# Reordering the opening and the schedule of a one-core hybrid attention layer: c turned alone, products of ones, and three ada chunks on TensorE

## The chip, the cores and the metric

The kernel runs on one core of one Trainium2 chip. The metric is the device time of one execution in microseconds. The core has five engines with instruction queues of their own: TensorE (PE), VectorE (DVE), ScalarE (ACT), GpSimd (POOL) and SyncE (SP), the last of which issues nearly all DMAs here. They meet at semaphores only.

## The reference

One layer on x (256 tokens by 1024) with a condition vector c. Everything is float32.

```python
mod = silu(c) @ ada_w + ada_b                     # 1024 x 3072
shift, scale, gate = split(mod, 3)
h = rmsnorm(x, pre_norm_w) * (1 + scale) + shift
mq, mk, mv, mg, dq, dk, dv, dz, db, da = split(h @ w_in)
mq, mk = partial_rope(mq), partial_rope(mk)
o_moba = attention(mq, mk, mv) * silu(mg)         # 8 heads of 64, causal
dq, dk, dv = split(silu(short_conv([dq, dk, dv])))
g = -exp(a_log) * softplus(da + dt_bias); beta = sigmoid(db)
o_dn = gated_delta_rule(dq, dk, dv, g, beta)      # 4 heads of 128, chunks of 64
o_dn = rmsnorm(o_dn, dn_norm_w) * silu(dz)
y = [o_moba, o_dn] @ w_out
out = x + gate * rmsnorm(y, post_norm_w)
```

With 256 tokens the block selection of the attention never picks another block, so it is plain causal attention. The delta rule needs, for each chunk of 64 tokens, the inverse of a lower triangular matrix, and then a recurrence over four chunks.

## The kernel before

Each engine's program is written out by hand as a list of calls of small functions (`hi(5)`, `qkv_products(3)`, `conv(2)` and so on); that list is the order of the work, and waits on semaphores stand in the functions. There is no scheduler.

**Products of high and low parts.** Every large product is done as three products of a reduced float32 type (`three`): high by high, high by low and low by high part. ScalarE rounds a unit of weights to its high part (`hi(n)`, into `whi`), POOL or VectorE takes the difference (`lo(n)`, into `wlo`; `DVE_LO` lists the units whose difference is VectorE's), and TensorE multiplies. There are 44 units: 0 to 15 for q, k, v of the delta rule (two for each of the eight 128-row chunks k of w_in, 768 columns), 16 to 35 for ten groups of 256 other columns of w_in (`half(j)`, two units a group, 1024 columns each), 36 to 43 for w_out (`y_products`). `whi` and `wlo` have four slots, `raw` has five; SP waits for the low part of the unit that had the slot before it loads the next.

**h by quarters.** The shift and scale columns of ada_w come in four quarters of 256 + 256 columns, each in eight chunks of 128 rows. VectorE multiplies the chunks by silu(c) and adds them up (`mod_sums(q, k0, k1)`), TensorE sums over the partitions with a column of ones (`mod(q)`), VectorE makes factor and offset (`modulate(q)`), ScalarE applies them to the turned x (`modulated(q)`) and rounds to `hhi`, VectorE makes `hlo` (`h_lo(q)`). The first quarter's chunks 6 and 7 go to TensorE directly, by one-column products (`mod_direct`, `DVE_K[0] = 6`). Then `qkv_products(2k)` and `(2k+1)` use chunk k of h.

**The opening.** SP loads c and four groups of parameter rows into `prow`, then the constants with the identity, then ada's first quarter, then units. TensorE turns all the rows together (L1252), VectorE copies them and makes the silu of c (L821 to L831), and only then starts `mod_sums(0, ...)`. ScalarE takes both squares of x. x is turned by TensorE (`x_turn`) into banks 0 to 3 and copied by ScalarE.

**After qkv.** VectorE runs the short convolution (`conv(m)`, L886), the gates (`gates_in`, `gates_out`), the silu and the ropes; TensorE meanwhile does the `half(j)` groups. The gated group `half(8)` needs bank and gate of an earlier group (`gate_done`). Then come the decay tables (`rows`, `row_sum`), the inverse in six levels (`z_products`, `mask_z`, `x_products`, `merge`, `t_turn`, alternately for token tiles 0 and 1), the attention heads in between, the recurrence (`vnew_products`, `state_products`, `state_update`), and the w_out products.

## Time and profile before

| | |
|---|---|
| three timed runs | 207.78, 210.75, 211.93 us (median 210.75) |
| profiled execution | 208.55 us, of it 206.5 us span |
| granted TensorE clock, mean | 0.994 |
| VectorE, ScalarE, POOL busy | 127.0, 105.9, 96.5 us |
| first weight product starts | 21.02 us |
| last matmul ends | 200.4 us |
| loaded from memory | 37.04 MB |

The page lists, for each group of instructions, the busy time, the mean of one in ns, and the idle time of its engine before it. In a timeline a row is: start in us, length in us, engine, line, operation, tile written <- tiles read, shapes, count, and in brackets the idle time before it with what ended it. Matmuls overlap, so the pace is read from their starts. A float32 matmul that is not of the reduced type stands as two instructions in the profile.

### The profile page before, as it was taken

To read this page: it belongs to the slowest core of one execution; us is meant where nothing else is said; L and a number is where in the kernel's file an instruction comes from. 1 tells how busy PE (TensorE), PEld (TensorE's weight loads), DVE (VectorE), ACT (ScalarE), POOL (GpSimd) and SP (SyncE) were. 2 spreads that over 40 slices of the span, in tenths; PEclk is the share of its full clock that TensorE was granted. 3 is DMA by queue.
4 is the path that set the end of the run, shared out by engine and by line. 5 is a ranking of instruction groups with operands and counts; after the bars stand their busy time and mean duration, and the time that the engine had idled before them with its cause. 6 is when DMAs were issued, how large, how long until landed. Compare 5 with 4: busy or idle time off the path is not lost.

```text
span 206.5 us, 4647 instructions
## 1 busy us (share of the span) xinstructions
PE 186.6 (90%) x1863; PEld 171.6 (83%) x1863; DVE 127.0 (61%) x306; ACT 105.9 (51%) x197; POOL 96.5 (47%) x51
## 2 busy tenths in 40 slices
PE   0079999999999989999999999999999999999980
PEld 0078999999999879999988999898999787788860
DVE  0634977752169988988586852677795135963055
ACT  4735573546476499965650445335251465545230
POOL 2003385687984927978642039701800480045400
PEclk9999999999999999999999999999999999999997
DMA  6999999994760587289247802450890094020022
GB/s 229 347 362 357 386 357 367 369 383 117 253 205 4 159 171 207 76 124 285 62 109 242 299 12 51 159 205 3 301 396 22 16 312 183 18 83 0 3 102 102
DMA packets 27881, 38.39 MB, mean 186 GB/s; under 512 B 2818, under 2 KB 21459, under 8 KB 27860
## 3 DMA queue, kind: packets, MB, share of 16 engines
q1 hardware_dynamic: 27572, 37.05, 55.6%
q10 hardware_dynamic: 288, 1.05, 1.4%
q8 instruction: 15, 0.25, 0.5%
q14 instruction: 6, 0.05, 0.1%
HBM read 37.04 MB, written 1.05 MB: 185 GB/s over the span
## 4 chain that ended last, share of the span: by engine, by line
PE 80%; DVE 10%; DMA 3%; SPq 2%; ACT 1%; issue 1%; POOL 1%; DVEq 0%; POOLq 0%
PE bank L1243 18%; PE bank L1245 16%; PE bank L1244 16%; DVE cv L886 6%; PE bank L1444 3%; DMA ada<-in_ada_w 3%; PE bank L1455 3%; PE bank L1432 2%; PE bank L1273 2%; PE bank L1266 2%; PE bank L1550 2%; PE bank L1526 2%; PE bank L1492 1%; SPq L322 1%; PE bank L1557 1%; PE bank L1503 1%
## 5 line engine op out<-in xcount | busy, mean ns | idle before, releaser
L442 POOL TENSOR_TENSOR wlo<-raw,whi 128x1024 fp32r<-128x1024 f32 (+1 forms) x30 | 69.6, 2338 | 75.7 <-ACT whi L520 75.7
L1243 PE MATMUL bank<-hhi,whi 128*128 128x256 f32 x224 | 66.0, 295 | 0.5 <-DVE hlo L837 0.5
L1244 PE MATMUL bank<-hhi,wlo 128*128 128x256 f32 x224 | 64.5, 288 | 0.0
L1245 PE MATMUL bank<-hlo,whi 128*128 128x256 f32 x224 | 64.5, 288 | 0.0
L1243 PEld LDWEIGHTS bank<-hhi,whi 128*128 128x128 f32 x224 | 44.1, 197 | 1.7 <-DVE hlo L837 0.9
L1244 PEld LDWEIGHTS bank<-hhi,wlo 128*128 128x128 f32 x224 | 44.2, 197 | 0.0
L1245 PEld LDWEIGHTS bank<-hlo,whi 128*128 128x128 f32 x224 | 44.0, 197 | 0.0
L520 ACT ACTIVATE whi<-raw 128x1024 fp32r<-128x1024 f32 (+1 forms) x33 | 32.8, 1026 | 15.7 <-DMA raw<-in_w_in 12.1
L886 DVE SCALAR_TENSOR_TENSOR cv<-bank,convh,cv 128x255 f32<-128x255 f32 (+2 forms) x36 | 17.0, 481 | 6.6 <-ACT cv L566 5.5
L865 DVE SCALAR_TENSOR_TENSOR bank<-ada,sml,bank 128x512 f32<-128x512 f32 x22 | 16.6, 753 | 0.6
L1243 PE MATMUL bank<-whi,ohi 128*128 128x512 f32 x32 | 12.8, 400 | 0.0
L1245 PE MATMUL bank<-wlo,ohi 128*128 128x512 f32 x32 | 12.5, 391 | 0.0
L1244 PE MATMUL bank<-whi,olo 128*128 128x512 f32 x32 | 12.5, 390 | 0.0
L635 ACT ACTIVATE pr<-bank,stat 128x128 f32<-128x128 f32 (+1 forms) x16 | 6.5, 418 | 11.3 <-DVE stat L1028 11.2
L1061 DVE SCALAR_TENSOR_TENSOR accg<-ada,sml,accg 128x512 f32<-128x512 f32 x16 | 12.0, 750 | 0.4
L456 POOL TENSOR_TENSOR rot<-rot,cst 128x512 f32<-128x512 f32 x4 | 5.2, 1290 | 14.3 <-DVE rot L1003 10.1
L442 POOL TENSOR_TENSOR wlo<-qkvs,whi 128x768 fp32r<-128x768 f32 x4 | 7.3, 1845 | 4.5 <-ACT whi L520 4.5
L1243 PE MATMUL bank<-whi,hhi 128*128 128x256 f32 x32 | 9.4, 293 | 0.0
L992 DVE TENSOR_TENSOR tt<-tt,bank 128x128 f32<-128x128 f32 x10 | 2.9, 287 | 10.1 <-PE bank L1455 10.1
L1244 PE MATMUL bank<-whi,hlo 128*128 128x256 f32 x32 | 9.1, 283 | 0.0
L1245 PE MATMUL bank<-wlo,hhi 128*128 128x256 f32 x32 | 9.1, 283 | 0.0
L643 ACT ACTIVATE pT<-bank 128x384 f32<-128x384 f32 x8 | 3.5, 489 | 10.4 <-PE bank L1557 10.4
(195 smaller groups left out, 348.8 us busy)
## 6 DMA issues: line engine op xcount, KB each, us to landing
raw<-in_w_in SPq DMA_DIRECT2D x20, 512.0 KB, 8.0
ada<-in_ada_w SPq DMA_DIRECT2D x32, 256.0 KB, 7.8
ada<-in_ada_w SPq DMA_DIRECT2D x4, 1024.0 KB, 12.0
raw<-in_w_out SPq DMA_DIRECT2D x8, 512.0 KB, 4.8
raw<-in_w_in SPq DMA_DIRECT2D x5, 384.0 KB, 7.3
qkvs<-in_w_in SPq DMA_DIRECT2D x4, 384.0 KB, 8.0
cv<-in_w_in SPq DMA_DIRECT2D x4, 384.0 KB, 8.6
xs<-in_x ACTq DMA_DIRECT2D x2, 512.0 KB, 3.9
```

The lines of the kernel that those rows point to most:

```text
L442: pool.tensor_tensor(split_u(wlo, n), raw_u(n), split_u(whi, n).bitcast(F32), ALU.subtract).then_inc(lo_done, 1)
L456: pool.tensor_tensor(rot[:, 1, :].rearrange("p (a s) -> p a s", a=2), rot[:, 0, :].rearrange("p (a s) -> p a s", a=2), cst[:, C_SIN:C_SIN ...
L520: act.activation(split_u(whi, n), raw_u(n), ACT.Copy).then_inc(hi_done, 1)
L635: act.activation(pr[:, e, o:o + w], bank[ATT[e]][:, o:o + w], ACT.Exp, scale=AD ** -0.5, bias=stat[:, 16 + i:17 + i], accum_out=stat[:, 32 ...
L865: link(dve.scalar_tensor_tensor(a, w, c_k, a, ALU.mult, ALU.add))
L886: ins = dve.scalar_tensor_tensor(cv[:, i, j:], b[:, 0:S - j], w, cv[:, i, j:], ALU.mult, ALU.add)
L1061: dve.scalar_tensor_tensor(a, ada0[:, k, :], sml[:, 24 + k:25 + k], a, ALU.mult, ALU.add).then_inc(gate_acc, 1)
L1243: pe.matmul(out, a[0][ia], b[0][ib], start=start, stop=False, skip_group_check=skip)
L1244: pe.matmul(out, a[1][ia], b[0][ib], start=False, stop=False, skip_group_check=skip)
L1245: return pe.matmul(out, a[0][ia], b[1][ib], start=False, stop=stop, skip_group_check=skip)
L1444: ins = pe.matmul(blocks(3 + 2 * t, 0, CHUNK)[r, h, :], tt[r, t * DH + h, :], ident_of(c), start=True, stop=True)
L1455: ins = pe.matmul(blocks(2 + 2 * t, 256, HALF)[r, h, :], ti[r, i, :], zt[r, i, :], start=True, stop=True)
```

## The change

It touches the opening and the lists of all five engines.

- **c alone.** c gets its own place (`crow`), is loaded first, with the constants right behind it, and is turned by itself (`c_turn`, bank 5). The silu is made from there. The other rows are turned later (`prow_turn`, bank 4, 73 rows).
- **Products of ones.** `busy(b, n)` issues n float32 products of the constant ones (128 by 128, by 256 columns) into a bank whose content is not used. There are 13 of them: 2, 3, 4 before the first ada products, and 4 before the last turn of x.
- **Three chunks on TensorE.** `DVE_K[0]` goes from 6 to 5. `mod(0)` now stands before `mod_direct(7)`, and `modulate(0)` waits for both.
- **First h by single chunks.** x turned goes to banks 3, 4, 5, 2. Quarter 0 is read straight from bank 3 and its two chunks of h stand in banks 6 and 7 (`h_home`), each with its own high and low part. VectorE squares one half of x, and copies the last turned block (`xT_move`) in ScalarE's place.
- **modulate** loses an instruction: factor and offset in one `scalar_tensor_tensor` for each column.
- **New orders** of loads and calls on every engine. `DVE_LO` goes from 3 units to 9. The ada quarters are loaded in halves between units.

```diff
-        DVE_K = (6, 8, 8, 8)
+        DVE_K = (5, 8, 8, 8)
+
+        XT_BANK = (3, 4, 5, 2)
+
+        def h_home(k):
+            return two(6 + k)[:, 0, :] if k < 2 else two(6 + k // 2 % 2)[:, k % 2, :]
...
-        DVE_LO = (2, 38, 40)
+        DVE_LO = (0, 12, 14, 21, 34, 37, 40, 41, 43)
...
             def modulated(q):
 
                 act.wait_ge(mod_read, q + 1)
-                act.wait_ge(xT_done, q + 1)
+                if q == 0:
+                    act.wait_ge(xT_ready, 1)
+                elif q < 3:
+                    act.wait_ge(xT_done, q)
+                else:
+                    act.wait_ge(xT_moved, 1)
+                k2 = slice(2 * q, 2 * q + 2)
                 for k in (2 * q, 2 * q + 1):
-                    act.activation(two(6 + q % 2)[:, k % 2, :], xT[:, k, :], ACT.Identity, scale=mod_a[:, k:k + 1],
-                                   bias=mod_b[:, k:k + 1]).then_inc(h_done, 1)
-
-            def h_hi(q):
-                act.wait_ge(h_done, 2 * q + 2)
-                act.activation(hhi[:, 2 * q:2 * q + 2, :], two(6 + q % 2), ACT.Copy).then_inc(hhi_done, 1)
+                    a = two(XT_BANK[0])[:, k, :] if q == 0 else xT[:, k, :]
+                    act.activation(h_home(k), a, ACT.Identity, scale=mod_a[:, k:k + 1], bias=mod_b[:, k:k + 1]).then_inc(h_done, 1)
+                    if q == 0:
+                        act.wait_ge(h_done, k + 1)
+                        act.activation(hhi[:, k, :], h_home(k), ACT.Copy).then_inc(hhi_done, 1)
+                if q > 0:
+                    act.wait_ge(h_done, 2 * q + 2)
+                    act.activation(hhi[:, k2, :], two(6 + q % 2), ACT.Copy).then_inc(hhi_done, 1)
...
+            def x_square():
+                dve.wait_ge(x_loaded[0], 16)
+                dve.tensor_tensor_reduce(xn[:, 0, :], xs[:, 0, :], xs[:, 0, :], 1.0, 0.0, ALU.mult, ALU.add, sml[:, 16:17]).then_inc(xms0_done, 1)
...
+            def xT_move(b):
+                dve.wait_ge(xT_ready, b + 1)
+                dve.tensor_copy(xT[:, 2 * b:2 * b + 2, :], two(XT_BANK[b])).then_inc(xT_moved, 1)
...
                 k2, b = slice(2 * q, 2 * q + 2), bank[mod_bank(q)]
                 dve.wait_ge(mod_ready, q + 1)
-                dve.tensor_tensor(b[:, 4:6], b[:, 2:4], scale1[:, k2], ALU.add).then_inc(mod_sum, 1)
+                if q == 0:
+                    dve.wait_ge(direct_done, NK - DVE_K[0])
...
+            def busy(b, n):
+
+                pe.wait_ge(ones_set, 1)
+                for _ in range(n):
+                    pe.matmul(bank[b][:, 0:256], ones[:, :], ones[:, 0:1].to_broadcast([P, 256]), start=True, stop=True)
+
+            def c_turn():
+                pe.wait_ge(c_loaded, 16)
+                pe.wait_ge(ident_loaded, 16)
+                pe.transpose(bank[5][:, 0:8], crow[0:8, :], ident[0:8, 0:8]).then_inc(c_turned, 1)
...
-                if k == 0:
-                    pe.wait_ge(xT_done, 3 if n == 0 else 4)
+                pe.wait_ge(hlo_done, h_part(k))
+                if n == 1:
+                    pe.wait_ge(hhi_done, 2)
+                    pe.wait_ge(xT_done, 2)
                 pe.wait_ge(*low_part(n))
                 for i in range(6 * (n % 2), 6 * (n % 2) + 6):
+                    if n == 0 and i == 4:
+                        pe.wait_ge(xT_moved, 1)
```

TensorE's list at the start of the program, before (th holds the turned rows, ada the first quarter's chunks, xn the scaled x):

```order
L1252 MATMUL bank<-cst,th 128x81
L1266 MATMUL bank<-sml,ada 128x1 x8
L1258 MATMUL bank<-cst,xn 128x128 x4
L1273 MATMUL bank<-ones,acc 128x1 x4
L1258 MATMUL bank<-cst,xn 128x128 x12
```

And the same place of the changed kernel, up to the first weight product:

```order
L1312 MATMUL bank<-ones 128x256 x2
L1317 MATMUL bank<-cst,th 128x8
L1312 MATMUL bank<-ones 128x256 x3
L1321 MATMUL bank<-cst,th 128x73
L1312 MATMUL bank<-ones 128x256 x4
L1340 MATMUL bank<-sml,ada 128x1 x8
L1348 MATMUL bank<-ones,acc 128x1 x4
L1340 MATMUL bank<-sml,ada 128x1 x4
L1332 MATMUL bank<-cst,xn 128x128 x12
L1312 MATMUL bank<-ones 128x256 x4
L1332 MATMUL bank<-cst,xn 128x128 x4
```

One turn became two, 13 products of ones came in, four more one-column products stand there, and the mod moved ahead of the last chunk and of all turns of x.

VectorE's list between the first four convolutions and the last two, before (qkvs is the silu, gcs the cumulated gates, ssq the sums of squares, rot and kT the second rope, the last row the first of conv(4)):

```order
L894 SCALAR_TENSOR_TENSOR qkvs<-th,cv 128x512 x2
L921 COPY gcs<-bank 128x32
L925 TENSOR_REDUCE ssq<-sq 128x4 x2
L1003 STREAM_SHUFFLE rot<-bank 128x512
L1004 TENSOR_TENSOR rot<-bank,cst 128x512
L1007 TENSOR_TENSOR kT<-rot 128x512
L925 TENSOR_REDUCE ssq<-sq 128x4 x2
L886 SCALAR_TENSOR_TENSOR cv<-bank,convh,cv 128x255
```

And of the changed kernel:

```order
L940 SCALAR_TENSOR_TENSOR qkvs<-th,cv 128x512 x4
L967 COPY gcs<-bank 128x32
L1049 STREAM_SHUFFLE rot<-bank 128x512
L1050 TENSOR_TENSOR rot<-bank,cst 128x512
L1053 TENSOR_TENSOR kT<-rot 128x512
L890 TENSOR_TENSOR wlo<-raw,whi 128x1024
L932 SCALAR_TENSOR_TENSOR cv<-bank,convh,cv 128x255
```

The sums of squares went behind the convolution, all four silu stand together, and a low part of 1024 columns came in. Not in these rows: `gates_in` now stands ahead of conv(3), and `rope(0)` directly behind it.

TensorE's list in the middle levels of the inverse, before (L1455 are x_products, L1444 t_turn, L1432 z_products, L1550 the scores of a pair of heads):

```order
L1455 MATMUL bank<-zt,ti 64x32 x8
L1444 MATMUL bank<-cst,tt 64x64 x8
L1432 MATMUL bank<-tt,am 64x32 x16
L1444 MATMUL bank<-cst,tt 64x64 x8
L1455 MATMUL bank<-zt,ti 64x32 x8
L1550 MATMUL bank<-kT,qT 128x128 x2
L1550 MATMUL bank<-kT,qT 128x256 x2
L1455 MATMUL bank<-zt,ti 64x32 x8
```

And of the changed kernel, levels 2 and 3 (L1534 x_products, L1523 t_turn, L1511 z_products, L1636 the turned probabilities):

```order
L1523 MATMUL bank<-cst,tt 64x64 x8
L1511 MATMUL bank<-tt,am 64x32 x8
L1523 MATMUL bank<-cst,tt 64x64 x8
L1511 MATMUL bank<-tt,am 64x32 x8
L1534 MATMUL bank<-zt,ti 64x32 x16
L1523 MATMUL bank<-cst,tt 64x64 x16
L1511 MATMUL bank<-tt,am 64x32 x16
L1534 MATMUL bank<-zt,ti 64x32 x8
L1636 MATMUL bank<-cst,pr 128x128 x6
```

Levels 1 to 3 now follow one another without other products between them; the `half` calls that stood among them went ahead of level 1 and behind the last `z_products`.

## Rows read from the trace of the kernel before

**Rows 1.** The page: busy time of each engine, its share, instructions.

```profile
PE 186.6 (90%) x1863; PEld 171.6 (83%) x1863; DVE 127.0 (61%) x306; ACT 105.9 (51%) x197; POOL 96.5 (47%) x51
```

**Rows 2.** The chain of waits, opening: start us, length us, what.

```profile
6.22 5.47 DMA ada<-in_ada_w
11.82 3.54 PE bank L1266 x16
15.37 0.95 PE bank L1258 x4
16.32 1.51 PE bank L1273 x8
...
18.25 1.07 ACT bank L547 x2
19.34 0.60 ACT hhi L552
...
20.04 0.70 DVE hlo L837
...
21.02 0.55 PE bank L1243
```

**Rows 3.** Windows: stretch, PE, PEld, DVE, ACT, POOL busy, PEclk, DMA share, GB/s.

```profile
21.00:26.00 5.00, 4.98 (x23) 5.00 (x24) 4.60 (x7) 2.44 (x4) 1.83 (x1) 1.00 1.05 384
31.00:41.00 10.00, 10.00 (x87) 10.00 (x86) 7.32 (x13) 4.59 (x7) 6.34 (x4) 1.00 1.07 367
71.00:81.00 10.00, 8.78 (x75) 8.51 (x74) 8.52 (x20) 8.22 (x16) 5.63 (x4) 1.00 0.89 205
```

**Rows 4.** Timeline of TensorE: the pace rises; a mod; a float32 product.

```profile
26.49 0.30 PE L1244 MATMUL bank<-hhi,wlo 128*128 128x256 f32 x1
...
27.82 0.95 PE L1273 MATMUL bank<-ones,acc 128*128 128x1 f32 x8
...
164.05 1.13 PE L1577 MATMUL bank<-accg,ones 128*128 128x512 f32 x2
```

**Rows 5.** Timeline of TensorE between 74 and 94 us.

```profile
76.87 0.36 PE L1358 MATMUL bank<-zz,cst 128*128 128x8 f32 x2 [0.85 <-DVE zz L916]
...
93.33 0.39 PE L1243 MATMUL bank<-hhi,whi 128*128 128x256 f32 x1
```

**Rows 6.** DMA issues of ada chunks 0, 5, 7: KB each, us to landing.

```profile
ada<-in_ada_w SPq DMA_DIRECT2D x1, 256.0 KB, 3.6
...
ada<-in_ada_w SPq DMA_DIRECT2D x1, 256.0 KB, 5.3
...
ada<-in_ada_w SPq DMA_DIRECT2D x1, 256.0 KB, 6.0
```

**Rows 7.** Timeline of VectorE: sums of quarter 0; low part of h chunks 2, 3.

```profile
9.26 2.32 DVE L865 SCALAR_TENSOR_TENSOR bank<-ada,sml,bank 128x512 f32<-128x512 f32 x3
...
31.06 0.69 DVE L837 TENSOR_TENSOR hlo<-bank,hhi 128x512 fp32r<-128x512 f32 x1 [0.37 <-ACT hhi L552]
```

**Rows 8.** Timeline of ScalarE: the high part of unit 0.

```profile
14.72 0.84 ACT L520 ACTIVATE whi<-raw 128x768 fp32r<-128x768 f32 x1 [3.16 <-DMA raw<-in_w_in]
```

**Rows 9.** Timeline of VectorE, 57 to 93 us: convolutions, rope's end, gate.

```profile
58.22 12.00 DVE L886 SCALAR_TENSOR_TENSOR cv<-bank,convh,cv 128x255 f32<-128x255 f32 x24 [5.53 <-ACT cv L566]
...
75.67 0.69 DVE L1007 TENSOR_TENSOR qT<-rot 128x512 f32<-128x512 f32 x1 [0.98 <-POOL rot L456]
...
92.09 0.69 DVE L1015 SCALAR_TENSOR_TENSOR gm<-th,bank 128x512 f32<-128x512 f32 x1 [0.72 <-ACT th L625]
```

**Rows 10.** Groups by line and form: busy us, mean ns, idle before.

```profile
L846 DVE TENSOR_TENSOR wlo<-raw,whi 128x1024 fp32r<-128x1024 f32 x2 | 2.4, 1222 | 0.2 <-ACT whi L520 0.2
```

**Rows 11.** The chain of waits, a level of the inverse on TensorE.

```profile
139.66 1.05 PE bank L1455 x32
...
141.51 1.08 PE bank L1444 x32
142.59 0.91 PE bank L1432 x32
```

More of the change, by code:

```diff
@@ L538, in xT_copy, with x_std, x_scale @@
+            def x_std():
+                act.wait_ge(xms0_done, 1)
+                act.wait_ge(xms1_done, 1)
+                act.activation(sml[:, 18:20], sml[:, 16:18], ACT.Sqrt, scale=1.0 / D, bias=epsc[:, 0:1]).then_inc(xstd_done, 1)
+            def x_scale():
+                act.wait_ge(xrstd_done, 1)
+                for t in range(NT):
+                    act.activation(xn[:, t, :], xs[:, t, :], ACT.Copy, scale=sml[:, 20 + t:21 + t]).then_inc(xn_done, 1)
             def xT_copy(b):
@@ L826, in _, with c_silu @@
[L826 to L837 removed]
+            def c_silu():
+                dve.wait_ge(c_tanh, 1)
+                link(dve.scalar_tensor_tensor(sml[:, 8:16], sml[:, 0:8], 1.0, bank[5][:, 0:8], ALU.add, ALU.mult))
+                dve.tensor_scalar(sml[:, 24:32], sml[:, 8:16], 0.5, None, ALU.mult).then_inc(sc_done, 1)
+                dve.wait_ge(sc_done, 1)
@@ new lines, in column_halves, with h_lo @@
+            def column_halves():
+                dve.wait_ge(pcol_done, 1)
+                dve.tensor_scalar(convh[:, :], pcol[:, R_CONV:], 0.5, None, ALU.mult)
+                dve.tensor_scalar(dnwh[:, :], pcol[:, R_DNW:R_DNW + 1], 0.5, None, ALU.mult)
+            def xT_move(b):
+                dve.wait_ge(xT_ready, b + 1)
+                dve.tensor_copy(xT[:, 2 * b:2 * b + 2, :], two(XT_BANK[b])).then_inc(xT_moved, 1)
+            def h_lo(p):
+                dve.wait_ge(hhi_done, p + 1)
+                if p < 2:
+                    k2, h = p, h_home(p)
+                else:
+                    k2, h = slice(2 * p - 2, 2 * p), two(6 + (p - 1) % 2)
+                dve.tensor_tensor(hlo[:, k2, :], h, hhi[:, k2, :].bitcast(F32), ALU.subtract).then_inc(hlo_done, 1)
@@ L1130, in _ @@
             mod_sums(2, 2, 4)
-            h_lo(1)
+            h_lo(2)
             mod_sums(2, 4, 8)
@@ L1135, in _ @@
             mod_sums(3, 2, 4)
-            h_lo(2)
+            h_lo(3)
             mod_sums(3, 4, 8)
             modulate(3)
-            h_lo(3)
+            lo(12)
+            h_lo(4)
+            lo(14)
             ba_lo()
@@ L1265, in mod_direct @@
                 for i in range(4):
-                    pe.matmul(bank[7][:, i:i + 1], ada[0][:, k, i * P:(i + 1) * P], sml[:, 24 + k:25 + k], start=(k == DVE_K[0] and i == 0),
-                              stop=False, skip_group_check=True)
+                    ins = pe.matmul(bank[7][:, i:i + 1], ada[0][:, k, i * P:(i + 1) * P], sml[:, 24 + k:25 + k],
+                                    start=(k == DVE_K[0] and i == 0), stop=False, skip_group_check=True)
+                ins.then_inc(direct_done, 1)
             def mod(q):
@@ L1610, in y_products @@
                     ins.then_inc(unit_done, 1)
+            busy(0, 2)
+            c_turn()
+            busy(1, 3)
+            prow_turn()
+            busy(3, 4)
+            mod_direct(5)
             mod_direct(6)
+            mod(0)
             mod_direct(7)
             x_turn(0)
-            mod(0)
             x_turn(1)
             x_turn(2)
+            busy(2, 4)
             x_turn(3)
```

464 lines of the change are left out of this document (236 added, 228 removed).

## The prediction

> **What bounds the kernel now.** I read four views. The page comes first: TensorE is busy 90% of the 206.5 us span [rows 1], so there is little idle time to win outside the ends, and the question is what TensorE waits for and how fast it runs. The chain of waits over the opening comes second [rows 2]. The first weight product starts at 21.02 us. Behind it stand a DMA (chunk 6 of the first ada quarter lands at 11.69), then 3.54 us of one-column products on TensorE, 0.95 us of transposes, 1.51 us of mod products, VectorE's three small operations, 1.07 and 0.60 us on ScalarE and 0.70 us on VectorE. TensorE is on this chain with 6.0 us, in products of one column. The windows by stage come third [rows 3]. From 21 to 26 us TensorE is busy all the time but starts only 23 matmuls, 0.217 us each; from 31 to 41 us it starts 87, 0.115 us each. The granted clock reads 1.00 in both rows, but 256 columns in about 0.213 us are the 1.2 GHz level and 256 in about 0.12 us are near the 2.4 GHz level (some matmul records are missing, so the paces are read a little slow or fast by a few ns), so I read the level from the pace. The eight one-column instructions of a mod take 1.51 us in the opening [rows 2] and 0.95 us (with the tail) inside the product stream [rows 4]. So the opening is slow twice: it is late, and it runs at the low level until about 26.5 us, where the first product shorter than 0.39 us stands [rows 4]. The last view is the timeline of VectorE and TensorE between 57 and 94 us. TensorE idles 0.85 us there behind VectorE's gate values [rows 5], and the window from 71 to 81 us has it busy for only 8.78 of 10 us [rows 3]. After it TensorE is full until 200 us.
>
> **What the change does, and its costs.**
>
> *Turning c alone.* Chunk 0 of ada is used at 7.6 us now because the silu of c waits for five small loads and the constants. c and the identity are now issued first, the silu is ready near 6 us, and VectorE can begin when chunk 0 lands (issued at 3.02 and 3.6 us under way [rows 6]: 6.6 us). VectorE gains x's first square, which the trace has not. A 512-wide operation takes 0.77 us [rows 7], so 1024 wide is 1.5 us by that row; it lies ahead of the silu, from x's landing near 4 to some 5.6 us, in idle time. VectorE then has five chunks instead of six and is done near 11.4 us. None of this is on the path, since chunk 7 lands only at 12.7 us: issued near 6.7 and 6.0 us under way; chunk 5, 5.3 us under way, lands at 11.0 [rows 6]. The ada loads start at the same time as before.
>
> *The products of ones.* Thirteen fp32 products of 256 columns, two instructions each. The gate product of 512 columns and two instructions takes 1.06 us at the high level (1.13 us with its tail [rows 4]), so one of 256 costs about 0.5 us at the high level and 0.85 at the low one. The first nine (2, 3 and 4) lie in idle time: 2 by 2.7 us, 3 from the identity's landing near 5 us to 7.7, 4 to at most 11.4. They keep TensorE streaming for about 6 us before chunk 5 lands. Now 5.5 us of full-width products (21.02 to 26.49 [rows 2, 4]) sufficed to raise the level, so I take it that the level is up when chunk 5's products start.
>
> *Three chunks on TensorE.* 8 instructions each. At the high level, 0.8 us, 0.95 with its tail [rows 4]; at the low one 3.54/2 = 1.77 us [rows 2]. High: chunk 5 from 11.1 to 11.9, chunk 6 to 12.7, mod to 13.5, chunk 7 to 14.3. Then 16 transposes at half of 0.24 us each (0.95 for four at the low level [rows 2]), 1.9 us, and four products of ones, 2.0 us: TensorE is ready at 18.1 us. The other side of the first product is modulate (14.7), the first units' high parts on ScalarE (the first one is done at 15.6 now [rows 8], the second about a unit's landing later, here 15.4), then per chunk 0.53 and about 0.35 us on ScalarE and 0.42 on VectorE: 16.8 us. TensorE is the later one, so the first product starts at **18.1 us instead of 21.02: 2.9 us**. The first 26 products at the high level save a further 26 x 0.10 = **2.6 us**.
>
> *What takes back.* First, products of the third tile wait for xT_moved, and VectorE gets to that copy only after two sums of quarter 1, whose loads now come behind a fourth unit: it ends near 20.3 us, products reach it at 19.5, **0.8 us** lost. Secondly VectorE: it starts quarter 1's six remaining sums at 20.5 and ends them at 25.2; then two sums of quarter 2 (26.8), modulate, 1.7 us on ScalarE, h_lo at 29.0 to 29.7. TensorE wants chunk 2 of h at 28.3 (18.1 + 0.8 + 72 x 0.119 + 0.8 for the mod), so it waits about **1.4 us**. Now this h_lo is done at 31.75 [rows 7] and the products reach it at 33.1, with room. For later quarters I find no wait: h for chunk 4 is ready at 37.9, wanted at 39.2; loads keep about 360 GB/s as now, when the DMA share is at its top (1.05 and 1.07 [rows 3]) and the last ada quarter lands near 40.2 us, its mod wanted at 43.5. So qkv ends 2.9 + 2.6 - 0.8 - 1.4 = **3.3 us** earlier.
>
> *Between 57 and 94 us.* VectorE runs this: 12.0 us for four convolutions, two more at the same price, ropes with a wait of 1 us each for POOL, the gate at 92.1 to 92.8 [rows 9]. The new order moves the convolution around the gates and puts lo(21) into it, one split of 1024 columns, 1.22 us [rows 10]. Now half(8) starts at 93.33 [rows 5] and needs the gate, done at 92.8, so there was 0.6 us of room. VectorE's work from the first convolution to the gate is 34.6 us now and 35.8 with lo(21): from 54.9 it ends at 90.7, where TensorE would be ready at 90.0. Of the 3.3 us, **0.7 us** goes, and 2.6 stay.
>
> *Later.* The inverse's levels now stand with less other work between them on TensorE. A level is 1.05 + 1.08 + 0.91 = 3.0 us of TensorE for both tiles [rows 11]; one tile's round is z 0.45, x 0.52, a mask and a merge on VectorE of about 0.3 us each and four hand-overs, some 2.1 us, which the other tile covers. I take nothing for it; if that cover fails, 0.5 us a level over four levels is 2 us. The moved splits (six more on VectorE, 6.8 us) lie in VectorE's idle 79 us (206.5 - 127.0 [rows 1]). The state chain and the y products keep their counts. I take nothing there either.
>
> *Sum.* The profiled execution took 208.55 us, 206.5 of it span. 208.55 - 2.6 = 205.95. The shown runs are 207.78, 210.75 and 211.93; the profiled one is among the faster of the four, their mean is 209.75. I set the sum on that mean: 209.75 - 2.6 = **207.2 us**, 1.7% under the median of 210.75.
>
> **The skill against the trace.** From 11.82 to 21 us TensorE does one-column products and transposes, and its pace stays at the low level: the first full-width products still take 0.217 us [rows 2, 3]. The Trainium skill, "TensorE: Matmul & The Clock Gate", Part 4, says that a transpose does not count as busy time for the clock. By that rule transposes and one-column products can lose what the ones gained between 11 and 16 us, although the engine is never idle. No row here shows a fall in such a stretch, only that there was no rise.
>
> **The rivals.**
>
> *A. The clock stays, or falls back, low (15%).* For: the stretch from 11.1 to 16 us is the very work that did not raise the level. Against: it comes right after 6 us of full-width work, and four products of ones stand among the transposes. If low throughout: three chunks and the mod take 7.1 us to 18.2, transposes 3.8, ones 3.4, first product at 25.4 us, 4.4 us later than now, with the cold products as now: 209.75 + 4.4 = **214 us**. It decides from the point where the level is low at chunk 5's first product. Falling only at the transposes costs 3.7 us of the gain and gives 210.5.
>
> *B. VectorE's stages do not bite (20%).* If the DVE order overlaps better (gate values done before the fourth convolution remove the 0.85 us wait [rows 5], and the wait at h chunk 2 is shorter), 4 to 5 us stay: **205.2 us**. Against: VectorE's work in the stage adds up as above.
>
> *C. New waits in the inverse or state part (23%).* Levels without cover, 2 us, or the last state step, where the tail of VectorE's queue is longer: **209.3 us**, or no change.
>
> **How the numbers follow.** My forecast (207.2, own range 206.2 to 208.3) has 42%, B 20%, C 23%, A 15%. From 203.8 (B with half a microsecond more and runs near the fast end) to 211.5 (C, and A's milder half) leaves out the rest of A and a little of B, under 2 in 10. About 2% is what a measurement of this kernel can tell from no change: faster means under 206.5. B gives nearly all of its 20%, the forecast's lower part 15%: 0.35. Slower, over 215, needs A in full and a slow draw: 0.10. The rest, 0.55.
>
> **What would show it.** Right: first product (bank from whi, hhi) near 18 us; one-column groups of 8 at 0.8 us; product pace 0.12 us from the start; one TensorE wait for hlo near 28 us; rows(0) behind VectorE's columns near 89 us; last product near 198 us. Wrong: one-column groups at 1.7 us (A), no wait near 28 us and half(8) before 90 us (B), idle TensorE between 105 and 150 us behind merges (C).

## The result, and the profile of the changed kernel

| | before | changed |
|---|---|---|
| timed runs, median (lowest to highest) | 211.13 us (207.78 to 211.93) | 222.21 us (220.28 to 226.33) |
| ratio | | 1.0644, 95% interval 1.0588 to 1.0699 |
| profiled execution, of it span | 208.55, 206.5 us | 221.17, 219.1 us |
| granted TensorE clock, mean | 0.994 | 0.955 |
| VectorE, ScalarE, POOL busy | 127.0, 105.9, 96.5 us | 143.5, 104.5, 83.9 us |
| last matmul ends | 200.4 us | 213.0 us |

The change costs 6.4%, where 1.7% of gain was forecast. Ratios below are to before on the same chip, and they leave out executions more than 1.5% above the fastest of their kernel.

TensorE's timeline over the opening and up to the first hand-over behind the qkv products (start, us, line, tiles, count, idle before with what ended it) answers [rows 2] and [rows 4]:

```profile
11.38 1.92 PE L1340 MATMUL bank<-sml,ada 128*128 128x1 f32 x16 [1.39 <-DMA ada<-in_ada_w]
13.16 1.03 PE L1348 MATMUL bank<-ones,acc 128*128 128x1 f32 x8
...
14.94 2.59 PE L1332 MATMUL bank<-cst,xn 128*128 128x128 f32 x12
17.33 2.53 PE L1312 MATMUL bank<-ones 128*128 128x256 f32 x8
19.70 0.60 PE L1332 MATMUL bank<-cst,xn 128*128 128x128 f32 x4
20.05 0.36 PE L1301 MATMUL bank<-hhi,whi 128*128 128x256 f32 x1
...
31.35 0.39 PE L1301 MATMUL bank<-hhi,whi 128*128 128x256 f32 x1 [1.10 <-DVE hlo L881]
...
45.28 0.95 PE L1348 MATMUL bank<-ones,acc 128*128 128x1 f32 x8
...
69.26 0.39 PE L1395 MATMUL bank<-cst,baT 16*128 16x16 f32 x2 [5.24 <-ACT baT L590]
```

The opening is recognisable: 16 one-column instructions in 1.92 us (3.54 before), the first product at 20.05 us (21.02 before), one wait for h chunk 2, and the last mod of the opening at 45.28 us, where it stood at 46.87. So 1.6 us are gained by then in this execution. The last row shows where they go: TensorE stands 5.24 us for `baT`. The windows by stage (stretch, TensorE busy and count, granted clock, DMA share, GB/s) answer [rows 3]:

```profile
15.00:21.00 6.00, 6.00 (x33) 0.72 1.07 360
...
51.00:61.00 10.00, 10.00 (x87) 1.00 0.30 85
61.00:71.00 10.00, 4.76 (x34) 0.77 0.54 190
71.00:81.00 10.00, 10.00 (x79) 0.89 0.55 77
81.00:91.00 10.00, 8.51 (x73) 1.00 0.49 136
...
101.00:111.00 10.00, 8.13 (x56) 0.83 0.33 102
111.00:121.00 10.00, 7.61 (x93) 0.83 0.17 57
121.00:131.00 10.00, 10.00 (x148) 1.00 0.01 2
```

Between 51 and 61 us the DMA engines are busy for 0.30 of the time (0.68 in before), and TensorE is idle for half of the window behind. The windows that hold the longest waits have a lower granted clock too (0.77, 0.83, 0.83), but not the one from 81 to 91 us, with 1.49 us idle at 1.00. Behind 121 us TensorE is full again (10.00 of 10 us, then 19.06 of 20 from 131 to 151, 19.92 in before): what is lost is lost between 60 and 121 us.

What kept the DMA engines idle stands in SyncE's queue. Its timeline (the length includes the wait in front of each issue), then GpSimd's and ScalarE's:

```profile
44.79 12.61 SPq L353 DMA_DIRECT2D raw<-in_w_in  x3
57.44 0.95 SPq L367 DMA_DIRECT2D cst<-in_consts  x1
...
54.05 2.40 POOL L461 TENSOR_TENSOR wlo<-raw,whi 128x1024 fp32r<-128x1024 f32 x1 [0.46 <-ACT whi L533]
...
67.89 1.06 ACT L533 ACTIVATE whi<-raw 128x1024 fp32r<-128x1024 f32 x1 [7.44 <-DMA raw<-in_w_in]
68.85 0.36 ACT L590 ACTIVATE baT<-bank 16x256 f32<-16x256 f32 x1
```

The three issues from 44.79 us are units 18, 21 and 19, in this order. Unit 21 takes `raw`'s slot of unit 16, so SyncE waits for the low part of unit 16, which GpSimd makes from 54.05 to 56.45. Unit 19, whose own slot is long free, stands behind it, then the constants and unit 20. Unit 19 lands at 67.9 us. ScalarE has waited 7.44 us for it with `hi(19)`, and `baT_copy`, which needs no load at all, stands behind `hi(19)`; for that TensorE and VectorE wait. In before's list unit 21 stands behind 16, 19, 20, 18 and 23.

VectorE and GpSimd near 108 us, and TensorE behind them (before: normalise 1.72 us for the same four):

```profile
108.71 5.21 DVE L1082 TENSOR_SCALAR pr<-pr,stat 128x128 f32<-128x128 f32 x4
...
108.63 4.68 POOL L461 TENSOR_TENSOR wlo<-raw,whi 128x1024 fp32r<-128x1024 f32 x2 [1.78 <-ACT whi L533]
...
106.99 0.36 PE L1301 MATMUL bank<-hhi,whi 128*128 128x256 f32 x1 [1.87 <-POOL wlo L461]
...
113.98 1.41 PE L1636 MATMUL bank<-cst,pr 128*128 128x128 f32 x6 [2.39 <-DVE pr L1082]
```

VectorE's four small operations lie over two splits of GpSimd and take three times as long as in before. That is a second suspect, with no row for it in the prediction.

### The profile page after: what moved, and what is told of

It reads as the page before. It is cut to its first block, busy times and chain, and to the rows that moved or that the text cites. A ratio compares the mean times of both kernels' runs of the same rounds, so it can differ in the third digit from the quotient of the medians.

```text
span 219.1 us, 4724 instructions
## 1 busy us (share of the span) xinstructions
PE 195.2 (89%) x1898; PEld 178.6 (82%) x1898; DVE 143.5 (65%) x315; ACT 104.5 (48%) x195; POOL 83.9 (38%) x45
## 4 chain that ended last, share of the span: by engine, by line
PE 58%; DMA 17%; DVE 8%; POOL 7%; SPq 4%; ACT 3%; issue 3%; DVEq 0%; POOLq 0%; ACTq 0%
DMA raw<-in_w_in 14%; PE bank L1301 10%; PE bank L1303 10%; PE bank L1302 10%; POOL wlo L461 7%; PE bank L1534 3%; DMA ada<-in_ada_w 2%; PE bank L1523 2%; DVE pr L1082 2%; PE bank L1511 2%; DVE bank L909 2%; ACT whi L533 2%; PE bank L1636 2%; PE bank L1605 1%; PE bank L1645 1%
## 5 line engine op out<-in xcount | busy, mean ns | idle before, releaser
L461 POOL TENSOR_TENSOR wlo<-raw,whi 128x1024 fp32r<-128x1024 f32 (+1 forms) x26 | 60.5, 2336 | 93.0 <-ACT whi L533 93.0
L533 ACT ACTIVATE whi<-raw 128x1024 fp32r<-128x1024 f32 (+1 forms) x33 | 33.3, 1025 | 26.0 <-DMA raw<-in_w_in 22.0
L909 DVE SCALAR_TENSOR_TENSOR bank<-ada,sml,bank 128x512 f32<-128x512 f32 x21 | 15.8, 752 | 1.2 <-DMA ada<-in_ada_w 0.7
L890 DVE TENSOR_TENSOR wlo<-raw,whi 128x1024 fp32r<-128x1024 f32 (+1 forms) x7 | 9.2, 1308 | 5.3 <-ACT whi L533 5.3
L1312 PE MATMUL bank<-ones 128*128 128x256 f32 x26 | 9.7, 533 | 1.1 <-DVE ones L845 1.1
```

The source lines that it names most:

```text
L461: pool.tensor_tensor(split_u(wlo, n), raw_u(n), split_u(whi, n).bitcast(F32), ALU.subtract).then_inc(lo_done, 1)
L533: act.activation(split_u(whi, n), raw_u(n), ACT.Copy).then_inc(hi_done, 1)
L890: dve.tensor_tensor(split_u(wlo, n), raw_u(n), split_u(whi, n).bitcast(F32), ALU.subtract).then_inc(dve_lo_done, 1)
L909: link(dve.scalar_tensor_tensor(a, w, c_k, a, ALU.mult, ALU.add))
L1312: pe.matmul(bank[b][:, 0:256], ones[:, :], ones[:, 0:1].to_broadcast([P, 256]), start=True, stop=True)
```

## The experiments

Two theories stand against each other, and against the prediction's rivals. **S, the queue:** loads that wait for a slot stand in front of loads that wait for nothing. **P, the held engine:** some of VectorE's operations that work from SBUF to SBUF are held while GpSimd splits.

### Unit 21 behind unit 20, and the other way about

In the changed kernel:

```diff
             load_unit(18)
-            load_unit(21)
             load_unit(19)
             load_constants()
             load_unit(20)
+            load_unit(21)
```

> The changed kernel with one line moved: load_unit(21) stands behind load_unit(20) instead of in front of load_unit(19). Theory S (SP's queue): unit 21 waits for the low part of unit 16, which is made at 56.5 us, and units 19, 20 and the constants stand behind it. Moved, unit 19 is issued near 46 us and, at the 8 us that such a load takes, is there before ScalarE asks for it (60.4 us). The 7.4 us wait of ScalarE, the 5.2 us wait of TensorE for baT and most of the later lag go: 9 to 13 us less than the changed kernel, 209 to 213 us. Theory O (the other new orders and the low parts on VectorE cost the time): 220 us or more, a gain of 2 us at most. Theory C (collisions of VectorE with POOL): about 218 us, since the collisions stay.

Measured: ratio 1.0121 (1.0070 to 1.0172). It rests on three of ten executions, 210.39 to 211.26 us; the other seven took 215.8 to 220.1, at nearly the same granted clock (0.963 to 0.973 against 0.970 to 0.973), and the profile is of one of them, 217.26 us. The median of all ten, 215.98 us, is 1.038 of before's. The wait for `baT` is gone in any case. So the one line gives back 5.2 points of the 6.4 by the short executions and 2.6 by all ten; that S carries most of the loss is settled by the next run and by the one with the queue alone mended. In the longer execution this is left, with 4.0 us in two waits for low parts (VectorE, GpSimd, TensorE):

```profile
104.48 5.19 DVE L1082 TENSOR_SCALAR pr<-pr,stat 128x128 f32<-128x128 f32 x4
...
104.38 4.67 POOL L461 TENSOR_TENSOR wlo<-raw,whi 128x1024 fp32r<-128x1024 f32 x2 [1.77 <-ACT whi L533]
...
109.72 1.54 PE L1636 MATMUL bank<-cst,pr 128*128 128x128 f32 x6 [3.85 <-DVE pr L1082]
```

The opposite edit in the kernel before: one load moved, nothing else.

```diff
             load_unit(16)
+            load_unit(21)
             load_constants()
             load_unit(19)
             load_unit(20)
             load_unit(18)
             load_unit(23)
-            load_unit(21)
```

> The kernel before with one line moved the other way: load_unit(21) directly behind load_unit(16), ahead of the constants and units 19, 20, 18. Theory S: unit 18, 19, 20 and the constants are held until the low part of unit 16 is made (58.6 us), so they land 8 us and more later, and TensorE stalls near 65 us: 5 to 12 us slower than before, 216 to 223 us. Theory O: no change, 211 us.

Measured: 1.0533 (1.0449 to 1.0618), all four executions at 218.6 to 221.1 us. The one line costs the kernel before most of what the whole change costs. TensorE's timeline, then SyncE's:

```profile
79.18 0.39 PE L1316 MATMUL bank<-cst,baT 16*128 16x16 f32 x2 [10.98 <-ACT baT L560]
...
42.25 16.41 SPq L340 DMA_DIRECT2D raw<-in_w_in  x2
```

Two issues take SyncE 16.41 us, and TensorE waits 10.98 us for the copy behind them.

### All loads of before; the copy ahead of hi(19)

With the changed kernel's loads from unit 12 on put back into before's order:

> The changed kernel with all loads from unit 12 on in the order of the kernel before; everything else as changed. Theory S: 208 to 211 us, since unit 25 in front of 22 to 24 and the late gate bias go too; the opening's gain of 1.6 us at the third mod is kept. Theory O: 219 us or more. If S holds but the new engine lists cost something on their own, this lands between: what is above 208 is their price.

Measured: 1.0233 (1.0123 to 1.0343), 213.0 to 219.5 us. The `baT` wait is gone, but before's order is not better here than the mended new one. What is left is a wait of 2.6 us for `zz`, and one of 2.2 us in the products of the inverse for which the trace has no releaser. In front of `zz` stands the plainest picture of P. VectorE, then GpSimd:

```profile
67.75 1.02 DVE L952 TENSOR_SCALAR zz<-sml 128x8 f32<-128x8 f32 x1
68.68 0.15 DVE L953 TENSOR_TENSOR zz<-sml,dab 128x8 f32<-128x8 f32 x1
68.87 2.27 DVE L954 SCALAR_TENSOR_TENSOR zz<-zz 128x16 f32<-128x16 f32 x1
...
63.97 7.14 POOL L461 TENSOR_TENSOR wlo<-raw,whi 128x1024 fp32r<-128x1024 f32 x3 [1.45 <-ACT whi L533]
```

The three splits, 2.38 us each, end at 68.73 and 71.11 us. The operations of 8 and 16 columns, 0.17 us where GpSimd is idle, end at 68.77 and 71.14: each is held to the end of a split. The two holds add up to some 2.9 us, about the wait for `zz`.

```diff
             hi(18)
-            hi(19)
             baT_copy()
+            hi(19)
```

> The changed kernel with ScalarE's baT_copy one place earlier, ahead of hi(19); the loads stay as changed. Theory S: unit 19 stays late, so half(1) stays late (its second unit's low part is made at 71.4 us), but VectorE's gates start near 66 instead of 69.7 us: 1 to 4 us less than the changed kernel. If the wait for baT alone were the loss, all of 5 us and more would come back.

Measured: 1.0685 (1.0573 to 1.0798), no gain over the changed kernel. The copy is made at 62.37 us, but the convolutions, the rope's table and the exponentials still stand behind units 19 and 20 and the constants; TensorE waits 4.8 us for `zz` and 3.9 for normalise. So here the late loads could not be made up for by a new order on the engine that waits for them.

### The opening alone

The changed opening, with every list behind it (SyncE from unit 12, ScalarE from `hi(13)`, VectorE from `ba_lo`, GpSimd from `lo(12)`, TensorE from `half(0)`) that of before:

> Only the opening of the change: c turned alone, the products of ones, three chunks of the first ada quarter on TensorE, h by single chunks, its loads up to unit 11; every order behind the qkv products (SyncE from unit 12 on, ScalarE from hi(13), VectorE from ba_lo, GpSimd from lo(12), TensorE from half(0)) is that of before. Prediction's sum: 3.3 us of gain at the end of the qkv products and 2.6 us at the end, so 0.985 to 0.99 of before. Theory S (the queue of loads stands behind unit 21, and the opening itself gives 1.6 us as the trace of after shows at mod(3)): 1 to 2 us faster than before, 0.990 to 0.997, first product near 20 us, baT turned near 67.5, last product near 199. Rival: the opening is where part of the loss comes from too (its ones and transposes leave the clock lower later): slower than before by 1% or more, with a granted clock under 0.97 behind the opening.

Measured: 0.9970 (0.9933 to 1.0006), 207.57 us, at the edge of what was expected and with an interval that touches 1. First product 19.55 us, last mod 44.77 (2.1 us earlier than before), `baT` 68.11 (0.8 earlier), last product 1.1 us earlier. TensorE's timeline:

```profile
10.88 1.92 PE L1340 MATMUL bank<-sml,ada 128*128 128x1 f32 x16 [1.25 <-DMA ada<-in_ada_w]
...
30.83 0.39 PE L1301 MATMUL bank<-hhi,whi 128*128 128x256 f32 x1 [1.11 <-DVE hlo L887]
...
68.11 0.29 PE L1395 MATMUL bank<-cst,baT 16*128 16x16 f32 x2 [0.79 <-ACT baT L596]
```

Of 2.1 us, 1.3 are lost by `baT`: `hi(18)` waits 2.76 us for its load. Without the thirteen products of ones:

> As e5, but all thirteen products of ones are left out (they compute nothing that is used). If they raise the clock as the prediction has it, chunk 5's products take 1.77 us for each eight (low level) instead of about 1.0, three chunks and the mod 7.1 us to about 18.4, transposes 3.8 us: first product 22 to 22.5 us against 20.0 with them, products of the first 26 at the low level (0.217 us): the whole about 2.5 to 4 us slower than e5. Rival (the ones cost as much as they bring, since four of them stand on the path behind the transposes): first product within 1 us of e5's, time within 1 us of e5's.

Measured: 1.0020 (0.9982 to 1.0058), 208.61 us, 1.0 us behind the run with them, though the two intervals overlap; 2.5 to 4 us were expected. The one-column products take 3.54 us for 16 and the first product comes at 20.87 us, less late than expected, since the four ones on the path (2.5 us) are gone too:

```profile
10.75 3.54 PE L1340 MATMUL bank<-sml,ada 128*128 128x1 f32 x16 [4.21 <-DMA ada<-in_ada_w]
...
17.57 3.65 PE L1332 MATMUL bank<-cst,xn 128*128 128x128 f32 x16
...
20.87 0.54 PE L1301 MATMUL bank<-hhi,whi 128*128 128x256 f32 x1
```

With the last four ones among the transposes (1, 1 and 2 of them between the four groups):

> As e5, but the four products of ones that stood together ahead of the last group of transposes stand among them: one behind the first group, one behind the second, two behind the third. If the level falls because transposes follow each other, 12 of them with nothing between (2.59 us at the low pace in the trace of after), full-width work among them keeps it: transposes at 0.12 us each, ones at 0.53 us, first product 1.5 to 2 us earlier than in e5. Rival (the level falls behind the one-column products already, or whatever stands there): the same first product as e5 within 0.4 us.

Measured: 0.9957 (0.9918 to 0.9996), 207.34 us. First product 19.40 us in the one execution profiled, 0.15 earlier: within the rival's 0.4 us.

```profile
14.29 0.63 PE L1332 MATMUL bank<-cst,xn 128*128 128x128 f32 x4
...
15.20 0.79 PE L1332 MATMUL bank<-cst,xn 128*128 128x128 f32 x4
...
16.64 1.06 PE L1332 MATMUL bank<-cst,xn 128*128 128x128 f32 x4
```

Here the level can be seen to fall: four transposes take 0.63, 0.79, then 1.06 us, although full-width ones stand between, and the granted clock is 0.50, the 1.2 GHz level, from 15.8 to 17.5 us. So the fall isn't undone by spreading the ones. It needs no transpose either: in the run with unit 21 behind 20, whose opening is the changed one, the granted clock is 0.52 from 13 to 14 us, and the mod's and chunk 7's one-column products are slow ahead of the first transpose (1.48 and 1.84 us for eight, 1.03 in the changed kernel's trace):

```profile
12.62 1.48 PE L1348 MATMUL bank<-ones,acc 128*128 128x1 f32 x8
13.96 1.84 PE L1340 MATMUL bank<-sml,ada 128*128 128x1 f32 x8
15.66 2.80 PE L1332 MATMUL bank<-cst,xn 128*128 128x128 f32 x12
```

The point at which the level falls and comes back moves from execution to execution, and with it the first product: in the 14 traces that have this opening with its ones, together or spread, it starts between 19.40 and 21.91 us, in eight of them later than the 21.02 us of before. Two traces 0.15 us apart tell nothing about the place of the ones.

### GpSimd's splits against VectorE's operations

As the first experiment (unit 21 behind 20), and:

```diff
             lo(26)
+            pool.wait_ge(pn_done, 1)
             lo(27)
```

> As the run with unit 21 loaded behind unit 20, but GpSimd's split of unit 27 waits until VectorE's normalise of the first head is done. Theory: VectorE's operation from SBUF to SBUF is held up while GpSimd splits (5.19 us for four of 128 columns there, 1.72 in before): normalise takes 1.0 to 1.8 us, TensorE's wait for it (3.85 us) falls under 1 us, and the first turn of probabilities comes 2.5 to 3.5 us earlier; the time up to 1.5% better than that run if nothing else waits next, or the same if TensorE then stands before the low parts of units 27 to 29. Rival (normalise is long for another reason): it still takes over 4 us.

Measured: 1.0136 (1.0079 to 1.0194), all four executions at 211.38 to 212.07 us. Normalise takes 1.01 us, no wait for it is left, and the window from 101 to 111 us is 10.00 us busy instead of 4.39. The times over 215 us of the first experiment (seven of ten) didn't appear; its short ones are not improved. This fits that the meeting made the long executions, but with four executions here and no trace of a short one there it isn't shown. VectorE and GpSimd at the gate values, in this run:

```profile
67.20 2.41 DVE L954 TENSOR_TENSOR zz<-sml,dab 128x8 f32<-128x8 f32 x1
69.65 0.17 DVE L955 SCALAR_TENSOR_TENSOR zz<-zz 128x16 f32<-128x16 f32 x1
...
67.19 2.41 POOL L461 TENSOR_TENSOR wlo<-raw,whi 128x1024 fp32r<-128x1024 f32 x1 [0.56 <-ACT whi L534]
```

The next three runs move the split of unit 20 off the gate values, by `pool.wait_ge(ba_abs, 1)` ahead of `lo(20)`: in the opening alone with spread ones, in the run above, and in before.

> As the opening alone with its ones among the transposes, but GpSimd's split of unit 20 waits until VectorE's gate values up to the absolute value are formed. In that run VectorE's operation on 128x8 elements took 1.57 us (0.17 where GpSimd is idle) and ended when GpSimd's splits ended. Theory of the held port: it takes 0.17 us, the gate values are ready 1.0 to 1.4 us earlier, TensorE's wait of 0.83 us for zz goes, and the time falls by 0.8 to 1.3 us, 0.990 to 0.993 of before. Rival (the split comes so late that GpSimd's rope product, or TensorE in front of the low part of unit 20, waits instead): the time is unchanged or up to 1 us longer.

> The changed kernel with unit 21 loaded behind unit 20, GpSimd's split of unit 27 behind normalise, and its split of unit 20 behind the gate values up to the absolute value. There VectorE's 128x8 sum was held 2.41 us, and TensorE waited 1.96 us for zz. Theory of the held port: the sum takes under 0.2 us, the wait for zz falls under 0.5 us, the clock stays up behind it, and 1.5 to 2.5 us are gained: 1.002 to 1.007 of before. Rival (VectorE's new order there is the bound, with convolution and rope ahead of the gate values): the wait stays over 1.2 us and the time within 0.7 us of that run (1.0136).

> The kernel before with one wait more: GpSimd's split of unit 20 behind the gate values up to the absolute value. In before the 128x8 operation took 1.44 us and TensorE waited 0.85 us for zz. Theory of the held port: the operation takes under 0.2 us, the wait goes, 0.5 to 1.0 us gained, 0.995 to 0.998 of before. Rival: the operation stays long (over 1 us), or TensorE waits elsewhere, and nothing changes.

Measured: 1.0235 (1.0149 to 1.0320), 1.0093 (1.0054 to 1.0133) and 1.0268 (1.0199 to 1.0338). In all three the gate operation takes 0.17 us, as P says. But in two of them the time rises by over 2% (1.0235 against 0.9957 without the wait, and 2.7% on before). VectorE and GpSimd in the first:

```profile
69.58 0.17 DVE L959 TENSOR_SCALAR zz<-sml 128x8 f32<-128x8 f32 x1
...
69.95 3.49 DVE L947 SCALAR_TENSOR_TENSOR qkvs<-th,cv 128x512 f32<-128x512 f32 x2
...
75.63 2.75 DVE L1060 TENSOR_TENSOR qT<-rot 128x512 f32<-128x512 f32 x1 [0.95 <-POOL rot L475]
...
70.11 2.78 POOL L461 TENSOR_TENSOR wlo<-raw,whi 128x1024 fp32r<-128x1024 f32 x1 [1.57 <-DVE zz L961]
...
75.49 2.34 POOL L461 TENSOR_TENSOR wlo<-raw,whi 128x1024 fp32r<-128x1024 f32 x1
```

The split now starts 0.16 us into the silu of q (1.29 us for the two elsewhere, 3.49 here; the split itself takes 2.78 instead of 2.41, so it is held too), and the next one 0.14 us ahead of the rope's last sum (0.69 elsewhere, 2.75 here). TensorE waits 3.9 us for `zz`, and the granted clock is 0.93 and 0.90 in the windows from 71 to 91 us. In before it is the same: `zz` 3.3 us, clock 0.90 and 0.76. Only in the run between them is the wait for `zz` gone (1.0136 to 1.0093, intervals that overlap, where 1.5 to 2.5 us were expected): there the split falls on convolutions. The rule was right and the remedy a matter of luck: one hold of 1.4 us became two of over 2. One added wait costs 2.7% on before; in that sum the two holds, the lower clock behind them and GpSimd's own delay (0.7 us of waits for low parts, none in before) stand together, so it is not the price of P alone.

The Trainium skill, "SBUF — State Buffer", "SBUF: two separate sides", has this: GpSimd and VectorE share a pair of ports under an exclusive lock, held for the whole instruction, and an operation of VectorE needs it if it has two SBUF inputs or runs in a mode that uses both ports. The trace agrees in both forms (two inputs `zz<-sml,dab`, 2.41 us; one input `pr<-pr,stat`, 5.21 us for four), and the single held operations on the gate values end with their split to within 0.05 us. Lying in SBUF alone does not hold an operation: in the first experiment's trace three sums with one input in SBUF take 0.62 us each (1.86 us for `ssq<-sq` from 83.25 us) in the middle of GpSimd's three splits from 83.08 to 90.64 us.

The loads of units 12 to 20 of the changed kernel, on top of the first of these three:

> As e9, with the loads of units 12 to 20 in the changed kernel's order (12, 13, 15, 16, 14, 17, 18, 19, 20, unit 21 in its old place behind 23). In the opening alone ScalarE waited 2.76 us for the landing of unit 18, and TensorE was busy 9.29 and 9.21 us of the two windows from 51 to 71 us. Theory: unit 18 lands 2 us or more earlier, TensorE is full from 51 to 71 us and reaches the gate sums 1 to 1.6 us earlier; VectorE then bounds, so half of it is kept: 0.5 to 1.0 us better than e9, about 0.987 to 0.99 of before. Rival (VectorE's stage is the bound already): the same time as e9, with a wait of 1 us or more for zz.

Measured: 1.0238 (1.0181 to 1.0296), the same as without, as the rival had it. TensorE is full from 51 to 71 us, as the theory had it, and then waits 4.3 us for `zz` instead of 3.9: VectorE bounds, and time won ahead of it is lost there.

### The second place in the queue, and what is left

The run with both splits later still has TensorE wait 3.3 us for low parts, and SyncE's order behind 20 is 21, 25, 24, 22, 23. Unit 25 waits for the low part of unit 20, made last of all, and 24, 22 and 23, which wait for those of 19, 17 and 18, stand behind it. In the order 21, 22, 23, 24, 25:

> As the run with both splits later (e10), but the loads behind unit 20 stand in the order 21, 22, 23, 24, 25 (in which their buffers come free) instead of 21, 25, 24, 22, 23. In e10 unit 25 waits for the low part of unit 20 (done near 69.3 us) ahead of 24, 22 and 23, whose buffers are free at 60.7 to 65.4 us, TensorE then waits 3.3 us in all for low parts (2.13 at 84.67) and the window 81 to 91 us shows 7.87 us busy at a granted clock of 0.83. Theory of the queue: both waits fall under 0.5 us in all, that window is over 9.5 us busy, and 2.5 to 4 us are gained on e10: 0.990 to 0.998 of before. Rival (VectorE or the transfers themselves bound there): waits for low parts stay over 2 us or turn into a wait for VectorE, and the time stays within 1 us of e10 (1.0093).

Measured: 1.0106 (1.0026 to 1.0187), where 0.990 to 0.998 was expected. The waits for low parts are gone, and nothing is gained. In VectorE's timeline, and GpSimd's:

```profile
85.36 2.87 DVE L942 SCALAR_TENSOR_TENSOR qkvs<-th,cv 128x512 f32<-128x512 f32 x1
...
79.75 7.94 POOL L461 TENSOR_TENSOR wlo<-raw,whi 128x1024 fp32r<-128x1024 f32 x3 [0.99 <-ACT whi L535]
```

The splits lie over the silu of the fifth tile (2.87 us; two of them took 1.29 elsewhere). It was held before this edit too (2.13 us), but there TensorE came later; now it waits 1.9 us for VectorE's `cols`. With ones among the transposes too:

> As e13, with the last four products of ones among the transposes. Theory: 0.2 to 0.5 us better than e13 (first product 0.3 us earlier, as in the opening alone), the best version if e13's expectation holds: 0.988 to 0.997 of before. Rival: no difference from e13 within 0.3 us, or slower, since any shift moves where GpSimd's splits meet VectorE's operations.

Measured: 1.0058 (1.0016 to 1.0099), not told apart from the run before (its interval overlaps) and short of the expected 0.988 to 0.997. And the changed kernel with its queue alone mended, no wait in GpSimd:

> The changed kernel with its queue of loads alone mended (21 behind 20, then 22, 23, 24, 25), and no wait added to GpSimd. If the queue is the whole loss: as e13, 0.990 to 1.0 of before in every run. If the held port is a cause of its own: splits of GpSimd still meet VectorE's sum for the gate values or normalise, the time is 1 to 3% above e13, or its runs fall in two groups 4 us or more apart as those of the run with unit 21 alone moved (210.4 to 211.3, and 215.8 to 220.1).

Measured: 1.0057 (1.0012 to 1.0101), all ten at 208.0 to 213.3 us with a median of 210.52, 1.010 of before's. So of the 6.4% the queue holds 5.9 points (5.5 by all ten), in the places of three loads: 21, 24 and 25. The expectation for P, 1 to 3% above the run before last, did not come: two waits in GpSimd bring nothing once the loads are on time. Last, the spread-ones opening with before's later lists and its loads in order of slots:

> The opening alone with its ones among the transposes (e7), and the loads behind unit 17 in the order 16, 18, 19, constants, 20, 21, 22, 23, 24, 25, 26 in place of 16, constants, 19, 20, 18, 23, 21, 25, 22, 24, 26. No wait is added to GpSimd. Theory of the queue alone: before had slack there, TensorE loses 1.6 us between 51 and 71 us to the late unit 18, VectorE bounds behind it, so 0 to 0.8 us better than e7 (0.992 to 0.996 of before). Theory of the held port: earlier loads move GpSimd's splits against VectorE's operations; if a split then lies over the sums of conv's tanh or a rope, the time is 2 to 6 us longer than e7, and VectorE's 128x512 operation there takes over 2 us.

Measured: 0.9938 (0.9892 to 0.9983), 207.43 us median of ten (206.13 to 209.55) against 208.52. It has the lowest ratio of all and is ahead of both kernels, by 0.6% over before; from the same opening with before's loads (0.9957) it is not told apart. The splits happen to miss the long sums (the gate operation takes 1.20 us, normalise 1.71; 1.44 and 1.72 in before). Its first product starts only at 21.38 us, so the gain is not the opening's alone.

## Why the prediction was wrong, point by point

**Turning c alone, ones, three chunks: right in the changed kernel's trace.** Chunk 5's products start at 11.38 us (11.1 predicted) at the high level, 16 in 1.92 us; mod(0) runs at 13.16 (12.7). The one-column groups were priced right: without the ones 16 take 3.54 us. But in the first experiment's trace, with the same opening, the level was down again at the mod (1.48 us for its eight).

**Transposes and the last ones: mis-sized.** 1.9 + 2.0 us were taken, at the high level; they took about 5.1 us with the granted clock at 0.72 between 15 and 21 us, and the first product came at 20.05 us instead of 18.1, with 21.91 us as the latest of the traces with this opening. This is the milder half of rival A, at 15% in all, whose own figures do not quite add up (3.7 us off 207.2 gives 210.9, not 210.5). The sentence of the Trainium skill ("TensorE: Matmul & The Clock Gate", Part 4) that a transpose doesn't count as busy time was quoted and given too little weight. The runs agree that the level falls around that stretch, but it can fall ahead of the first transpose, among one-column products, of which that sentence does not speak. The 26 products behind it did run at the high level (0.36 us for the first, 0.55 before), so the 2.6 us term stands.

**The wait at h chunk 2: right,** 1.10 us against 1.4. The 0.8 us for `xT_moved` did not come: TensorE has no gap between 20.05 and 26.49 us. The gain at the last mod of the opening was 1.6 us in the changed kernel and 2.1 in the opening alone, against 3.3 at the end of the qkv products; the first product's 1.95 us are most of what is missing, and some 0.5 us more go around mod(1) and the wait at chunk 2.

**"VectorE runs this", between 57 and 94 us: the step that failed.** The sum let VectorE alone bound that stretch and took the arrival of units 18 to 25 at nothing, without a reason. "Loads keep about 360 GB/s" was said of the ada quarters, where it holds (360 to 371 GB/s in the windows from 15 to 41 us), and nothing was said of the loads behind them: from 51 to 61 us they moved 85 GB/s. In its place the runs show TensorE waiting 5.24 us for a copy that stands behind unit 19's load, which stands behind SyncE's wait for the low part of unit 16. Two facts were at hand and not put together: which slot each load waits for, and when GpSimd makes the low part that frees it. In before no unit up to 20 stands behind the wait for unit 16's low part; in the changed list 19, the constants and 20 do. The edit was one of many moved lines of the diff, and no term was made for SyncE. Unit 21's place cost 5.3% on the kernel before and up to 5.2 points in the changed one (2.6 by all ten executions); with units 22 to 25 in order it was 5.9.

**The 0.7 us for VectorE in that stretch: right in kind, too small.** In the opening alone 1.3 us go by `baT`, to loads; in the run with the first loads early VectorE takes all of what is won. What was missing in the sum is that VectorE's durations depend on GpSimd: its 34.6 us were carried over from before's trace with the hold that lay in them (1.44 us for the gate operation), as if a new order left it as it was. In the runs the gate operation took from 0.17 to 2.41 us, and the silu of two tiles 1.29 or 3.49.

**Later, the inverse and state (rival C): not there** as described. In the changed kernel TensorE is full behind 121 us but for 0.9 us. With the queue mended one wait is seen there, 1.7 us in the products of a pair of heads, with no releaser in the trace. In all, the new orders behind the opening cost about 1% (1.0057 with them and the queue mended, 0.9938 to 0.9970 with before's); how it divides over the moved calls is open.

**The range** ended at 211.5 us. Its slower side held the clock and the inverse only; no rival was made of a queue.

## What to carry to other kernels

For every load that a change moves, write down what its issue waits for and what stands behind it in the same queue, and take the time of that releaser from the trace; a load that waits for a slot is best put behind those that wait for nothing. Then ask who shares the waiting engine's list: a 0.36 us copy that needs no load stopped TensorE for 5 us. For the VectorE operations that were seen held here, the duration beside an idle GpSimd is only a lower bound, and any shift in time moves where the two meet: of three runs that held back the same split, two made two worse meetings of one. And a first product read from a single trace of each kernel is no measure of an opening when the same opening starts it anywhere within 2.5 us.

## What the runs showed of the hardware

- An operation of VectorE on 8 columns took 2.41 us, to within 0.05 us to the end of GpSimd's 2.41 us split beside it. Convolutions with an operand in a bank aren't held: 14 in 6.95 to 6.96 us, 0.50 each, beside three splits (before: 0.50 each). Nor are sums with one input in SBUF: three in 1.86 us beside a split.
- Idle time of TensorE costs again behind it: with 5.24 us of waiting the granted clock was 0.77 in the window that holds it and 0.89 in the next, and in the kernel before with one wait more 0.90 and 0.76 around 3.3 us; there TensorE started 65 matmuls from 81 to 91 us, 85 in before.
- The level can fall to 1.2 GHz while TensorE is not idle: from 12 us on it had no pause, and the granted clock went from 1.00 to 0.50 among one-column products and transposes behind full-width ones, at 13 us in one execution and at 15 in another of the same opening, and was back at 1.00 between 18 and 22 us.
- A load of 512 KB of w_in takes 8.0 (before) and 8.5 us (changed) from issue to landing, medians of 20 on the pages. Unit 19, issued once unit 21's slot came free at 56.45 us, landed at 67.9.
